# Latents' norm by logarithm and exponential with the index keys' norm behind it, and one and a half DeltaNet gate tiles at the RWKV seam in place of unread matmuls

## What is computed

```python
def rms_norm(x, g, eps=EPS):
    return x * lax.rsqrt(jnp.mean(x * x, axis=-1, keepdims=True) + eps) * g

# MLA
c_q = rms_norm(c_q, q_norm)           # 256 wide
c_kv = rms_norm(c_kv, kv_norm)        # 256 wide
k_I = layer_norm(k_I, kI_g, kI_b)     # index keys, 64 wide
...
# mixers joined; the second term is DeltaNet's
g_a, g_b, g_c = _split(jax.nn.sigmoid(p_g), (D_MODEL, D_MODEL, D_MODEL))
x = x + (g_a * y_a + g_b * y_b + g_c * y_c) @ w_mix_out[l]
```

## Time and profile before

| | |
|---|---|
| median of three runs | 2725.36 us (2717.42 to 2725.80) |
| the profiled execution's own time | 2714.44 us |
| its span | 2712.3 us |
| PE busy | 2469.7 us, 91% of the span |
| DVE busy | 1898.1 us, 70% |
| ACT busy | 1601.2 us, 59% |
| chain that ended last | PE 51%, DVE 34%, ACT 8%, issue 6% |
| mean granted TensorE clock | 0.980 of full speed |

### The profile page before, as it was taken

The page is one execution under the profiler, slowest core; times in us unless marked ns, Lnnn a source line. Parts: engine busy times, 40 slices in busy tenths (PEclk is TensorE's granted clock), DMA queues, the critical chain, the costliest instruction groups (busy, mean ns, idle before and its releaser), DMA issues.

```text
span 2712.3 us, 68677 instructions
## 1 busy us (share of the span) xinstructions
PE 2469.7 (91%) x30242; PEld 2044.9 (75%) x30250; DVE 1898.1 (70%) x2256; ACT 1601.2 (59%) x2162; POOL 355.6 (13%) x180
## 2 busy tenths in 40 slices
PE   6998999999999999989999999978989899898987
PEld 6766766778767777766667877778888888888887
DVE  6666564335355566676643354489999999999998
ACT  5454345343453344534453334578888888888886
POOL 0000001000000000000020000013243323332331
PEclk9999999999999999999999999999999999999999
DMA  6411221133446444211311333389999999999996
GB/s 220 148 48 49 64 63 41 59 106 111 139 154 217 157 149 121 93 49 33 94 32 41 109 117 124 124 306 388 385 387 391 388 383 385 385 389 386 385 389 230
DMA packets 304056, 531.43 MB, mean 196 GB/s; under 512 B 18544, under 2 KB 145776, under 8 KB 303376
## 3 DMA queue, kind: packets, MB, share of 16 engines
q1 hardware_dynamic: 303616, 525.99, 55.0%
q10 hardware_dynamic: 144, 1.05, 0.1%
HBM read 524.91 MB, written 2.10 MB: 194 GB/s over the span
## 4 chain that ended last, share of the span: by engine, by line
PE 51%; DVE 34%; ACT 8%; issue 6%; DMA 0%; POOLq 0%; POOL 0%; ACTq 0%; DVEq 0%; SPq 0%
DVE arena L3011 24%; PE bank L898 10%; PE bank L749 5%; PE bank L1419 4%; PE bank L1372 4%; PE bank L779 3%; PE bank L1435 2%; DVE yacc L3019 2%; PE bank L918 2%; PE bank L859 2%; PE bank L869 2%; PE bank L688 2%; PE bank L783 1%; PE bank L791 1%; PE bank L1523 1%
## 5 line engine op out<-in xcount | busy, mean ns | idle before, releaser
L3011 DVE TENSOR_TENSOR arena<-ring,arena 128x2048 bf16<-128x2048 f32 x334 | 829.5, 2528 | 1.3 <-ACT arena L2229 1.3
L2229 ACT ACTIVATE arena<-ring 128x2048 bf16<-128x2048 f32 x334 | 636.9, 1912 | 96.2 <-DMA ring<-in_moe_w_down 26.7
L1523 PE MATMUL bank<-arena 128*128 128x0 bf16 x10752 | 494.3, 210 | 97.6 <-DVE arena L3011 92.3
L1523 PEld LDWEIGHTS bank<-arena 128*128 128x128 bf16 x10752 | 482.1, 100 | 110.4 <-DVE arena L3011 100.2
L1673 POOL TENSOR_TENSOR arena<-yacc,arena 128x512 bf16<-128x512 f32 x112 | 298.4, 2675 | 957.3 <-ACT arena L2252 957.3
L898 PE MATMUL bank<-feat,ring 128*128 128x256 f32 x1408 | 366.3, 398 | 10.0 <-ACT arena L1735 4.9
L898 PEld LDWEIGHTS bank<-feat,ring 128*128 128x128 f32 x1408 | 256.7, 194 | 73.0 <-issue 26.2
L1540 PEld LDWEIGHTS bank<-arena 128*128 128x128 bf16 x5376 | 238.1, 98 | 21.2 <-issue 20.2
L1540 PE MATMUL bank<-arena 128*128 128x0 bf16 x5376 | 245.0, 206 | 6.3 <-issue 4.3
L1742 ACT ACTIVATE arena<-bank 128x256 f32<-128x256 f32 (+1 forms) x164 | 72.6, 443 | 209.4 <-PE bank L749 85.6
L1650 POOL TENSOR_TENSOR arena<-arena 64x512 f32<-64x512 f32 x16 | 22.4, 1401 | 1022.9 <-ACT arena L1882 857.0
(11 more groups left out here) (402 smaller groups left out, 3998.7 us busy)
## 6 DMA issues: line engine op xcount, KB each, us to landing
ring<-in_moe_w_gate SPq DMA_DIRECT2D x112, 1024.0 KB, 8.3
ring<-in_moe_w_up SPq DMA_DIRECT2D x112, 1024.0 KB, 7.7
ring<-in_moe_w_down SPq DMA_DIRECT2D x112, 1024.0 KB, 8.2
ring<-in_w_in SPq DMA_DIRECT2D x76, 1024.0 KB, 5.2
ring<-in_xa_w_kv SPq DMA_DIRECT2D x16, 1024.0 KB, 5.7
ring<-in_ffn_w_gate SPq DMA_DIRECT2D x11, 1024.0 KB, 5.3
ring<-in_ffn_w_up SPq DMA_DIRECT2D x11, 1024.0 KB, 5.8
ring<-in_ffn_w_down SPq DMA_DIRECT2D x11, 1024.0 KB, 6.0
```

The lines of the kernel that those rows point to most:

```text
L1523: m = mm(o, w[k // 4][wi][:, k % 4, col:col + P], xg[:, e % 2, xi, k, :].shape_from_register(width[e % 2]), start=i == 0 and k == 0, stop= ...
L2229: sc.activation(w_parts[b][0], ring[:, b * FFN_SLOT:(b + 1) * FFN_SLOT], ACT.Copy).then_inc(S["w_hi"], 1)
L3011: v.tensor_tensor(w_parts[b][1], ring[:, b * FFN_SLOT:(b + 1) * FFN_SLOT], w_parts[b][0], ALU.subtract).then_inc(S["w_lo"], 1)
```

## The change

At the seam, PE's five unread matmuls go. After the wait for `gn_y`, four steps (one tile) of DeltaNet gate work are taken, and after the decays' transposes and the wait for the convolved inputs two more (half a tile). On ACT the copy of that first tile stands between the decays and the sigmoid of the RWKV gates. In the latents' norm, DVE makes the latents' variance as soon as its sums are there; ACT takes logarithm and exponential (scale -0.5) of it in place of root and reciprocal; DVE scales the latents; and only then does the index keys' variance follow, by the same two functions. The four unread matmuls go. ACT's table for logarithm and exponential is loaded ahead, behind the DeltaNet gates' sigmoid.

```diff
@@ PE, end of rwkv
                 fill(side, 4)
-                unread(5, 1)
                 pe.wait_ge(S["gn_y"], c.need("gn_y"))
@@ PE, gdn
             def gdn(l):
+                side = gate_and_latent_beside()
+                fill(side, 4)
                 pe.wait_ge(S["gd_g"], c.need("gd_g"))
...
                 second = front_gd(range(4, 8), GD_BUFS[0])
-                side = gate_and_latent_beside()
+                fill(side, 2)
@@ PE, mla
                 for _ in keys:
                     pass
-                unread(4, 4)
                 pe.wait_ge(S["ml_n"], c.need("ml_n"))
@@ ACT, end of rwkv
                 decays(l)
+                side = gate_and_latent_beside()
+                fill(side, 4)
                 gates(gate_rw)
+                return side
@@ ACT, gdn
                 second = front_gd(l, range(4, 8), GD_BUFS[0])
-                side = gate_and_latent_beside()
+                fill(side, 2)
...
                 gates(gate_gd)
+                sc.preload_act_table_set("natural_log_exp_and_others")
                 fill(keys, 5)
@@ ACT, mla
             def mla(l, keys):
+                act.wait_ge(S["ml_ms"], c.need("ml_ms"))
+                act.wait_ge(*c.last())
+                sc.activation(mt[:, 2:4, :], mt[:, 0:2, :], ACT.Ln).then_inc(*c.inc("act_step"))
+                act.wait_ge(*c.last())
+                sc.activation(mt[:, 2:4, :], mt[:, 2:4, :], ACT.Exp, scale=-0.5).then_inc(*c.inc("ml_sd"))
                 fill(keys, 2)
                 act.wait_ge(S["ml_ms"], c.need("ml_ms"))
                 act.wait_ge(*c.last())
-                sc.activation(mt[:, 5, :], mt[:, 4, :], ACT.Sqrt).then_inc(*c.inc("ml_sd"))
-                act.wait_ge(S["ml_ms"], c.need("ml_ms"))
+                sc.activation(mt[:, 5, :], mt[:, 4, :], ACT.Ln).then_inc(*c.inc("act_step"))
                 act.wait_ge(*c.last())
-                sc.activation(mt[:, 2:4, :], mt[:, 0:2, :], ACT.Sqrt).then_inc(*c.inc("ml_sd"))
+                sc.activation(mt[:, 5, :], mt[:, 5, :], ACT.Exp, scale=-0.5).then_inc(*c.inc("ml_sd"))
@@ DVE, mla
                 v.tensor_tensor(mt[:, 0:4, :], cqk, cqk, ALU.mult).then_inc(*c.inc("ml_sq"))
                 dve.wait_ge(*c.last())
+                dve.wait_ge(S["ml_ss"], c.need("ml_ss"))
+                v.tensor_scalar(mt[:, 0:2, :], bk(2).rearrange("p (a b) -> p a b", a=2), 1.0 / 256, EPS,
+                                  ALU.mult, ALU.add).then_inc(*c.inc("ml_ms"))
+                dve.wait_ge(*c.last())
                 dve.wait_ge(S["kI_m"], c.need("kI_m"))
...
                 v.tensor_tensor(mt[:, 4, :], kI, kI, ALU.mult).then_inc(*c.inc("kI_v"))
                 dve.wait_ge(*c.last())
+                dve.wait_ge(S["ml_sd"], c.need("ml_sd"))
+                for i in range(4):
+                    gain = pc(l, "q_norm", i) if i < 2 else pc(l, "kv_norm", i - 2)
+                    v.scalar_tensor_tensor(cqk[:, i, :], cqk[:, i, :], gain, mt[:, 2 + i // 2, :], ALU.mult, ALU.mult).then_inc(*c.inc("ml_n" if i == 3 else "dve_step"))
+                    dve.wait_ge(*c.last())
                 dve.wait_ge(S["kI_m"], c.need("kI_m"))
                 v.tensor_scalar(mt[:, 4, :], bk(3, T, T), 1.0 / 64, EPS, ALU.mult, ALU.add).then_inc(*c.inc("ml_ms"))
...
-                v.reciprocal(mt[:, 4, :], mt[:, 5, :]).then_inc(*c.inc("dve_step"))
-                dve.wait_ge(*c.last())
-                v.scalar_tensor_tensor(kI, kI, pc(l, "kI_g"), mt[:, 4, :], ALU.mult, ALU.mult).then_inc(*c.inc("dve_step"))
+                v.scalar_tensor_tensor(kI, kI, pc(l, "kI_g"), mt[:, 5, :], ALU.mult, ALU.mult).then_inc(*c.inc("dve_step"))
...
-                dve.wait_ge(S["ml_ss"], c.need("ml_ss"))
-                dve.wait_ge(S["ml_sd"], c.need("ml_sd"))
-                v.reciprocal(mt[:, 0:2, :], mt[:, 2:4, :]).then_inc(*c.inc("dve_step"))
-                dve.wait_ge(*c.last())
-                for i in range(4):
-                    gain = pc(l, "q_norm", i) if i < 2 else pc(l, "kv_norm", i - 2)
-                    v.scalar_tensor_tensor(cqk[:, i, :], cqk[:, i, :], gain, mt[:, i // 2, :], ALU.mult, ALU.mult).then_inc(*c.inc("ml_n" if i == 3 else "dve_step"))
-                    dve.wait_ge(*c.last())
```

More of the change, by code:

```diff
@@ L2045, in recur_gd, with gdn @@
                     yield
-            def gdn(l):
+            def gdn(l, side):
                 sc.preload_act_table_set("natural_log_exp_and_others")
@@ L2339, in _ @@
                 mix_high(l, 2)
-                rwkv(l)
-                mla(l, gdn(l))
+                mla(l, gdn(l, rwkv(l)))
                 residual_high(l, -12, yacc)
@@ L2830, in mla @@
                 dve.wait_ge(*c.last())
-                v.tensor_scalar(mt[:, 0:2, :], bk(2).rearrange("p (a b) -> p a b", a=2), 1.0 / 256, EPS,
-                                  ALU.mult, ALU.add).then_inc(*c.inc("ml_ms"))
-                dve.wait_ge(*c.last())
                 dve.wait_ge(S["ml_sd"], c.need("ml_sd"))
-                v.reciprocal(mt[:, 4, :], mt[:, 5, :]).then_inc(*c.inc("dve_step"))
-                dve.wait_ge(*c.last())
-                v.scalar_tensor_tensor(kI, kI, pc(l, "kI_g"), mt[:, 4, :], ALU.mult, ALU.mult).then_inc(*c.inc("dve_step"))
+                v.scalar_tensor_tensor(kI, kI, pc(l, "kI_g"), mt[:, 5, :], ALU.mult, ALU.mult).then_inc(*c.inc("dve_step"))
                 dve.wait_ge(*c.last())
```

## The result

| | before | changed |
|---|---|---|
| median | 2727.19 us (12 runs) | 2733.43 us (12 runs) |
| lowest to highest | 2717.42 to 2735.47 | 2726.30 to 2745.90 |
| profiled execution | 2714.44 | 2732.77 |

The ratio is 1.0025 with a 95% interval of 1.0013 to 1.0036: the changed kernel is 0.25% slower, some 7 us, where I had forecast 3.5 us less. The median lies outside my range, 2711 to 2730. The single profiled executions differ by 18 us, and most of that must not be explained: the first 380 us of layer 0 hold the same instructions in both, but for the five unread matmuls at their very end, and still take 4.0 us longer (L2634 starts at 377.61 before and, as L2641, at 381.63 now). So all that follows is read as stretches between two instructions, not as points of time.

A forecast was written before the change was run, and what follows sets the result against it. PE, busy nine tenths of the span though partly not usefully, was taken to set the end. Per layer -4.47 (norm), +2.4 (seam) and +0.3 (tail), twice, gave -3.5 us: 2725.4 to 2721.9 us, range 2711 to 2730.

The forecast's parts named there:

- The latents' norm: Norm ends five microseconds early and PE goes straight on from the last key tile: gain 4.47 us per layer.
- The rival in which nothing of the gain arrives: A transfer due at a set time behind the norm eats its gain, leaving seam and tail: 2731 us; chance 0.05.
- The seam's chain: From `gn_y` to the fronts: ACT's sigmoid waits behind its copy of PE's tile, so the first front starts 3.05 us later.
- The seam's clock: At the seam low clock costs +2.5 per layer, 1.65 of it in the tile; whole seam +2.4, bounds -0.15 to +4.9.
- 0.9 for half a chance of a second fall: At the fronts behind the seam's tile: the clock may fall once more, priced +0.9 us per layer.
- regained by clock: Fronts at full clock win back three microseconds lost at the seam's head, leaving the seam at -0.15 us per layer.
- The tail: Last recurrence and behind, where six steps of side work are missing: +0.3 us per layer, bounds -2 and +2.
- -0.7 won: In the last recurrence: L1234 starts earlier, no longer behind side work, gaining 0.7 us per layer.
- +1.0 of clock: Behind the last recurrence: PE idles 3.9 us and key tiles may start at half clock, costing 1.0 us per layer.
- The inversions: Tile boundaries shift by half a tile, as many as before: cost 0, bounds of half a microsecond per layer.
- my third rival: Half tile shifts all boundaries so ACT's copy falls behind a front's chain: 24 us more, 2746 us; chance 0.10.
- the first is out: First rival: the clock holds at the seam and in the tail, total -10.6 us, some 2715 us; chance 0.24.

The follow-up runs named there:

- the norm alone: Only the latents' norm part of the change, with the seam as in the kernel before: ratio 0.9969 against the kernel before, median 2716.40 us.
- all three mended: Changed kernel with five unread matmuls back at the seam, ACT's tile copy behind the sigmoid, and four unread matmuls in the tail: ratio 1.0002, median 2727.54 us.
- the mended kernels: Two kernels: all three mended (ratio 1.0002 against the kernel before), and the same without the half tile ahead of the fronts (0.9996).
- ACT's swap: Changed kernel with ACT's copy of the first gate tile moved behind the RWKV gates' sigmoid: ratio 1.0024 against the kernel before, median 2733.19 us.
- the unread matmuls at the seam: Changed kernel with the five unread matmuls put back ahead of the wait for `gn_y`: ratio 1.0042 against the kernel before, median 2737.13 us.
- the kernel with the fronts held: The norm alone plus two unread matmuls in the fronts of heads 0, 1 and 3: ratio 0.9921 against the kernel before, median 2706.21 us.
- seam alone: Only the seam part of the change, with the latents' norm as in the kernel before: ratio 1.0070 against the kernel before, median 2747.43 us.
- mended, no half tile: All three mended, without the half tile of side work ahead of the fronts: ratio 0.9996 against the kernel before, median 2722.72 us.

## Why the prediction was wrong, point by point

**The latents' norm: right.** Its sum was 4.47 us per layer; the table has 4.5, and the norm alone measures 8.5 us in all. The norm ends five microseconds early, ACT's copy of the key tile is not held up, and no transfer is waited for. The rival in which nothing of the gain arrives is out by two comparisons, 8.5 and 12 us, though the interval of the first alone reaches down to 1.

**The seam's chain: right.** ACT's sigmoid waits for PE's tile; L1840 starts 4.8 us later counted from `gn_y` (before 1.2 us behind it, now 5.9). The first L1154 was forecast at 8.35 plus 1.65 for the clock, and came at 10.06. The second came at 14.11, against 12.3 + 1.65. What the chain left unsaid is that PE's tile and a half alone holds the first sum back by 2 us: with ACT's copy out of the way and a fast tile it came at 7.29, not at 5.3.

**The seam's clock: undersized.** I took +2.4 per layer for the whole and it is +3.7. The term that fell short is "0.9 for half a chance of a second fall". In every profiled seam of the changed kernel the second sum and most of the half tile behind it ran at the low level; in three of four the tile had too, and in the fourth the first sum. With the whole of it in the sum, layer 0 of the first profile is met: 19.5 + 1.65 for the tile + 0.95 for the second sum + 0.85 for the half tile (2.8 us for 1.9) is 22.95, and 22.86 was measured. The other 0.4 of the difference lies in the kernel before: I had read its longest seam, 19.65, and the mean of four is 19.3. The larger error stands behind this: three microseconds lost at the head were to be "regained by clock", and the seam has the same 10 us at the low level as before.

**The tail: the step that failed.** The forecast was +0.3 per layer, from -0.7 won and +1.0 of clock, with bounds of 2; measured is +3.2. The -0.7 was right: without low clock the tail is 24.75 us (all three mended) against 25.39 in the layers of the kernel before without it. So the failed term is the +1.0 of clock, which measures +3.9 (3.2 and the 0.7 won). I had priced only the clock behind the recurrence, where PE idles, and taken the time within the recurrence from rows at full clock. I had not asked what the shift by six steps puts into the recurrence: no more tiles of dense matmuls but L943, eight columns wide. That falls are needed for this loss is shown by the mended kernels, whose tails are 24.7 to 25.5 us. What brings them is not shown. PE counts as busy for 6.0 of the 6.0 us from 1500 to 1506, and the clock falls right behind, so it is no idle time just ahead; but with all three mended the same thin matmuls in the same place ran at full clock, so it isn't they alone either.

**The inversions: wrong at 0.** "As many boundaries as before" was true and beside the point: what matters is beside which of ACT's chains a boundary falls. Two fell badly, 1.88 and 1.03 us against 0.72 and 0.79, +1.4 per layer, and with the falls of the clock it is +2.0, outside my bound of 0.5. This was my third rival; its mechanism is there, in two places per layer instead of eleven. Its condition (0.16 us more per boundary turns the sign) was met only with the falls counted in: 1.4 over eleven boundaries is 0.13, 2.0 is 0.18. Its price of 24 us was also a slip: 1.1 us of waiting against 0.47 is 0.63 more, 14 us in all.

**The sum.** By its own steps: 2 x (-4.5 + 3.7 + 2.0 + 3.2) = +8.8 instead of 2 x (-4.47 + 2.4 + 0 + 0.3) = -3.5. The tail is off by 2.9, the inversions by 2.0 and the seam by 1.3, each of them dearer than forecast. The rivals: the clock did not hold, so the first is out; nothing of the norm's gain was lost. The range failed because the bounds of the single terms were never added up on the dear side: -4.2 for the norm, +4.9 for the seam, +2 for the tail and +0.5 for the inversions made 2 x 3.2 and so 2732, beyond the upper end of 2730 that I wrote, and still a microsecond short of the measured median.

The rule that I cited of the Trainium skill (TensorE: Matmul & The Clock Gate, "HAM oscillation — how this bites in real kernels") was right for the tile in three of the four profiled seams of the changed kernel. There the trace agrees: 5.41 us for what takes 3.62. In the fourth it does not: behind the same 3.35 us of idle time the tile took 3.72 us. Of all fourteen profiled seams with no unread matmuls ahead of the tile, four are of this kind.

**What stays open.** Why ACT's swap and the unread matmuls at the seam, each of which shortens its own stretch, gave nothing in the total: in their profiles the recurrences and the tail are longer by about as much, and the fall of the clock there may depend on when they are reached, but no run held the one fixed while it moved the other. For the same reason it is open what brings the falls in the tail, and why the three edits together keep it at full clock. Nor is it settled whether the expert layer's stretch, from cross attention to the end, 1005 and 1007 us in the kernel before and 1008 and 1009 in the changed one, is scatter: the kernel with the fronts held has 1010 there and is the fastest. Of that kernel's gain over the norm alone only a small part is in the profiled stretches. And the fastest kernel was not tried with the tail held as well.

## What to carry to other kernels

Moving work to where an engine idles takes it from where it was: follow every later step that shifts, and ask what each place then holds, what chain each wait falls beside, and whether what is left keeps the clock. Put nothing that waits for another engine's new work ahead of a link of the chain: ACT's copy ahead of the sigmoid held the first sum back by 1.1 us, though the swap alone gave nothing in the total. And read a stretch in two profiles or more, beside stretches that the change doesn't touch, before a cause is put to a microsecond. Last, a change that only takes away a wait (the norm) is worth keeping apart from one that trades places: timed together they hid a gain of 0.3%.

## What the runs showed of the hardware

The scatter of this kernel's time goes with the clock. Over the 35 runs of the kernel before that were timed beside the first four experiments, the time at the low level and the time of the run have a correlation of 0.96, and a run with one microsecond more at the low level is 0.43 us longer. Over the 29 runs beside the next four it is 0.83 and 0.33 us, over the 17 beside the last 0.93 and 0.36 us. (The time at the low level is twice the span times what the mean clock lacks to 1.) The kernels differ in the same way:

| kernel | runs | mean clock | us at the low level | mean time, us |
|---|---|---|---|---|
| before | 35 | 0.9764 | 129 | 2726.5 |
| norm alone | 12 | 0.9762 | 130 | 2717.7 |
| changed | 12 | 0.9718 | 154 | 2734.4 |
| seam alone | 12 | 0.9709 | 160 | 2747.0 |
| mended, no half tile | 12 | 0.9762 | 129 | 2721.7 |
| fronts held | 6 | 0.9813 | 101 | 2706.6 |

At 0.43 us each, the 25 us more at the low level in the changed kernel than in the norm alone would make 11 of the 16.7 us between them, at 0.33 only 8; the rest would be waiting. The 29 us less with the fronts held would give 9 to 12, and 11.1 were measured, with twelve more unread matmuls in the list. The chips of these kernels were not all the same, and the clock of a run is known to three digits, 5 us at the low level, so this is a rough estimate and no cause shown. I had not expected the clock to fall right behind 6 us in which PE's row is full.
